# A transformer block on one core: weight splits ahead of the normalised input, the query's square ahead of the forget scan, and sums of squares two steps later

## The reference

```python
h = rms_norm(x, norm1_g)
z = h @ w_in                          # 512 pool, 512 q, 512 k, 512 v, 8 forget columns
log_f = log_sigmoid(z_f + b_forget)
q, k = rms_norm(q, q_norm_g), rms_norm(k, k_norm_g)       # per head, 8 heads of 64
y_pool = pool_mixer(z_pool, w_pool, pool_scale)           # trailing means over 2, 4, 8, 16 frames
F = cumsum(log_f, axis=1)
s = q @ k.T / sqrt(64) + F[t] - F[s]                      # causal, softmax, times v
x = x + concat([y_pool, y_attn]) @ w_out
x = x + peer_ffn(rms_norm(x, norm2_g), w_query, peer_sub_keys, expert_u, expert_v)
# peer_ffn: 8 retrieval heads, product keys, top 16 of 16384 experts per head,
# softmax gates, y = sum g_e * gelu(u_e . h) * v_e
```

## Time and profile before

| | |
|---|---|
| median of 3 runs | 1567.3 us (1561.99 to 1569.34) |
| span of the profiled execution | 1569.7 us; its time around the span is not listed apart |
| TensorE busy | 1513.6 us, 96% |
| DVE, ACT, POOL busy | 1156.7, 602.9, 973.6 us |
| mean granted clock of TensorE | 0.983 of full speed |
| chain that ended last | PE 79%, DVE 7%, ACT 5%, DMA 5%, issue 4%, POOL 1% |
| first 230 us | TensorE busy 200.1 us |

### The profile page before, as it was taken

How to read it: one execution, slowest core, us unless ns; L and a number is a source line. 1 busy time by engine, 2 the same in 40 slices (tenths; PEclk the granted TensorE clock), 3 DMA queues, 4 the chain that set the end, 5 groups by cost and what they waited for, 6 DMA issues and landing times.

```text
span 1569.7 us, 20625 instructions
## 1 busy us (share of the span) xinstructions
PE 1513.6 (96%) x7613; PEld 1323.5 (84%) x7613; DVE 1156.7 (74%) x1938; ACT 602.9 (38%) x808; POOL 973.6 (62%) x525
## 2 busy tenths in 40 slices
PE   6899999899999999999999999999999999999999
PEld 4655567688999999999899999998888888888887
DVE  5467754317899999819899889848777777777774
ACT  5557533433333333344343344433333333333332
POOL 2321133433578878666576667658878878888784
PEclk9899999999999999999999999999999999999999
DMA  4311111322467777568999998699888988888883
GB/s 154 108 67 47 49 54 68 118 77 81 144 214 251 271 262 258 197 223 276 352 334 334 357 361 300 236 355 396 325 348 318 348 348 316 350 322 343 348 296 121
DMA packets 117974, 381.53 MB, mean 243 GB/s; under 512 B 11416, under 2 KB 27928, under 8 KB 117408
## 3 DMA queue, kind: packets, MB, share of 16 engines
q1 hardware_dynamic: 70096, 202.64, 35.7%
q0 software_dynamic: 36864, 134.23, 23.3%
q10 hardware_dynamic: 10960, 44.06, 7.1%
HBM read 336.84 MB, written 44.06 MB: 243 GB/s over the span
## 4 chain that ended last, share of the span: by engine, by line
PE 79%; DVE 7%; ACT 5%; DMA 5%; issue 4%; POOL 1%; ACTq 0%; SPq 0%; DVEq 0%
PE bank L623 24%; PE bank L624 24%; PE bank L625 24%; DMA picked<-u_dram,picks 4%; PE bank L824 4%; ACT wh L428 1%; PE bank L768 1%; POOL wl L401 1%; DVE rinv L931 1%; DVE hl L884 1%; PE bank L639 1%; ACT L512 1%; DVE pr L1034 1%; DVE pad L1004 1%; PE bank L720 1%
## 5 line engine op out<-in xcount | busy, mean ns | idle before, releaser
L401 POOL TENSOR_TENSOR wl<-raw,wh 128x1024 fp32r<-128x1024 f32 x211 | 522.1, 2475 | 470.6 <-ACT wh L428 469.1
L623 PE MATMUL bank<-hh,wh 128*128 128x384 f32 (+1 forms) x1184 | 428.2, 362 | 7.1 <-DVE hl L884 7.1
L624 PE MATMUL bank<-hl,wh 128*128 128x384 f32 (+1 forms) x1184 | 415.4, 351 | 0.0
L625 PE MATMUL bank<-hh,wl 128*128 128x384 f32 (+1 forms) x1184 | 414.5, 350 | 0.0
L624 PE MATMUL bank<-wl,Wh 128*128 128x512 f32 x768 | 300.7, 392 | 0.0
L623 PE MATMUL bank<-wh,Wh 128*128 128x512 f32 x768 | 300.0, 391 | 0.0
L625 PE MATMUL bank<-wh,Wl 128*128 128x512 f32 x768 | 298.4, 389 | 0.0
L428 ACT ACTIVATE wh<-raw 128x1024 fp32r<-128x1024 f32 x225 | 236.7, 1053 | 151.7 <-PE bank L625 138.7
L623 PEld LDWEIGHTS bank<-hh,wh 128*128 128x128 f32 x1184 | 225.3, 190 | 17.1 <-DVE hl L884 7.4
L624 PEld LDWEIGHTS bank<-hl,wh 128*128 128x128 f32 x1184 | 225.4, 190 | 9.6 <-issue 1.7
L625 PEld LDWEIGHTS bank<-hh,wl 128*128 128x128 f32 x1184 | 224.8, 190 | 9.0
(11 more groups left out here) (164 smaller groups left out, 1759.7 us busy)
## 6 DMA issues: line engine op xcount, KB each, us to landing
raw<-uT_dram SPq DMA_DIRECT2D x128, 512.0 KB
xraw<-v_dram SPq DMA_DIRECT2D x72, 512.0 KB
raw<-v_dram SPq DMA_DIRECT2D x56, 512.0 KB
a_dram<-act_a ACTq DMA_DIRECT2D x64, 384.0 KB
wf<-a_dram SPq DMA_DIRECT2D x32, 768.0 KB, 6.9
raw<-wst_dram SPq DMA_DIRECT2D x41, 512.0 KB
gates_dram<-gbuf ACTq DMA_DIRECT2D x4, 4096.0 KB, 16.6
gt<-gates_dram SPq DMA_DIRECT2D x32, 512.0 KB
```

Source lines behind the costliest of these rows:

```text
L401: pool.tensor_tensor(wl[:, n % SPLIT, :], raw_of(n), wh[:, n % SPLIT, :].bitcast(F32), ALU.subtract).then_inc(w_lo, 1)
L623: pe.matmul(dst, ah, bh, start=start, stop=False)
L624: pe.matmul(dst, ah, bl, start=False, stop=False)
L625: return pe.matmul(dst, al, bh, start=False, stop=stop)
```

## The change

Three edits, in the list of steps and in ACT's program:

1. In `norm1`, ACT splits weight chunks up to 4 ahead of the first copy into `mh`, chunk 5 ahead of the fourth and chunk 6 ahead of the seventh; before, it had chunk 3 ahead of the fifth and chunks 4 to 6 behind the last. The numbers in `hi_to` are the last chunk to be split by then.
2. In a query or key chunk, ACT's square comes directly behind the copy, and only then the wait for the forget scan with its DMA (first chunk), or the wait for the stored rows with the loads of `nf` (second).
3. `ss` and `norm` of a chunk lie at pieces 2 and 3 of the next projection instead of 0 and 1.

```diff
         def sums(i):
 
-            return [(0, "ss", i), (1, "norm", i)]
+            return [(2, "ss", i), (3, "norm", i)]
...
                         act.activation(zc[:, z % 2, :], bank[bank_of(n)][:, :], ACT.Copy).then_inc(zc_ready, 1)
+                        if kind(n) == "qk":
+                            act.wait_ge(zc_ready, z + 1)
+                            square(SQ_QK + z, zc[:, z % 2, :])
                         if n == QK_W[0]:
                             act.wait_ge(f_done, 1)
                             act.dma_start(f_dram, fg[:, 2, :]).then_inc(f_stored, 16)
...
                             for h in range(2):
                                 forget(h)
-                        if kind(n) == "qk":
-                            act.wait_ge(zc_ready, z + 1)
-                            square(SQ_QK + z, zc[:, z % 2, :])
...
                     for k in range(KD):
-                        if what == "norm1" and k in (0, 4):
-                            hi_to(2 + k // 4)
+                        if what == "norm1" and k in (0, 3, 6):
+                            hi_to(4 + k // 3)
                         act.wait_ge(h_ready, base + k + 1)
```

## The result

The changed kernel takes 1580.4 us (median of 4 runs, 1579.3 to 1582.3), against 1568.3 for the kernel before: ratio 1.0078, interval 1.006 to 1.0097. It is slower by more than the 0.5% that can be told from no change, by some 12 us. The span of the profiled execution went from 1569.7 to 1580.5, +10.8, the mean granted clock from 0.983 to 0.978.

The account below looks back on a forecast made before the run. It took three chains, none TensorE's own, to decide; the heads' cycle closes on ACT and DVE. 0 - 4.9 + 2.0 + 1.1 + 7.8 + 0.8 = +6.8 on a 1569.7 span, 1576.5; as median 1574, range 1561 to 1583.

Parts of the forecast that it names:

- rival A: Heads: clock drops at the transposes make TensorE the bound; +12.3 us, about 1580, chance 0.24.
- Edit 1 brings nothing: First normalisation: four POOL meetings delay ml to 49.8, the forget scan ends as before, 0 us.
- The square ahead of the scan, the key 4.9 us sooner: Query and key chain: var starts right behind the scan, -3.5 us; -4.9 in all, key ready at 78.1.
- helps once more: Query and key chain: edit 3 lets the second var follow the first norm, key gain from 3.5 to 4.9 us.
- Half clock behind the first key, +2.0: First scores of head 0: a 3.8 us wait for the key brings half clock, costing 2.0 us.
- Head 0, +1.1: Head 0: the second mask is ready 0.6 us behind pT instead of 1.45, costing 1.1 us.
- Heads 1 to 4, +1.95 each: Heads 1 to 4: two Exps ahead of the table load delay root and norm 1.95 us each, +7.8.
- with a late sum behind a half clock: Upper end for the cost in heads 1 to 4: +3.0 us a head.
- 0.8 for all clock effects: Heads: clock drops from TensorE idling 2.3 us a head taken as +0.8 us in all, ends 0 and +7.
- waits for `pr` of about 2 us a head: Sign that the forecast is right: TensorE waits about 2 us a head for pr in heads 1 to 4.
- more than two half-clock stretches between 100 and 190 us: Sign in the trace that would make the outcome rival A.
- Behind the heads, no change: From head 5 on: order and lengths unchanged, so the shift goes through to the end.

Follow-up runs that it names:

- Experiment 4: Only the earlier weight splits in norm1, on the kernel before: 1569.6 us, ratio 1.0003.
- experiment 1: The changed kernel with sums and norms back at pieces 0 and 1, so edits 1 and 2 without edit 3: 1561.5 us, ratio 0.9969.
- experiment 5: The changed kernel with TensorE's sums back at piece 0, ACT and DVE keeping the late order: 1573.0 us, ratio 1.0033; a mirror kernel was run too.
- experiment 8: Two kernels with edits 1 and 2, late sums only for chunks 0, 1 and 3, or only in heads 0 to 4: 1564.1 and 1574.3 us.
- experiment 2: Only the sums and norms moved to pieces 2 and 3, on the kernel before: 1583.5 us, ratio 1.0098.
- the mirror of experiment 5: The changed kernel with TensorE's sums late at piece 2, but ACT and DVE in the order of before: 1574.4 us, ratio 1.005.
- the first of experiment 8: Edits 1 and 2, with late sums only for chunks 0, 1 and 3, outside and ahead of the heads: 1564.1 us, ratio 0.9985.
- experiment 7: Edits 1 and 2 with early sums, and the scaling of the values moved behind the forget projection: 1566.5 us, ratio 0.999.
- experiment 3: Only ACT's square moved directly behind the copy, on the kernel before: 1562.7 us, ratio 0.997.
- the second of 8: Edits 1 and 2, with late sums only in heads 0 to 4, those of chunks 0, 1 and 3 early: 1574.3 us, ratio 1.0067.

## Why the prediction was right and wrong

The time was in the range (1561 to 1583) and the direction was said, but the forecast, 1574 and "no change", was not what happened: rival A, slower by the clock, was, at the 1580 that it named, though mostly in other places than it said. That its number came out is in part luck: at head 5's Exp the kernel was 14.1 us late, where A had 12.3, and 3.4 came back behind it.

- *Edit 1 brings nothing.* Right. Four meetings with POOL, the last `ml` at 49.48 for 49.8, the scan at 60.84 for 61.4. Experiment 4 shows the zero by itself.
- *The square ahead of the scan, the key 4.9 us sooner.* Right, 5.6. But of this edit 3's share was taken as "helps once more", and beside edit 2 it doesn't: with early sums the key is ready at 77.27 to 77.73 (experiments 1, 5 and 8), with late ones at 77.24 to 77.38. Only without edit 2 does it bring 2.5 us (experiment 2). The copy right behind the split, which I counted for edit 3, comes of edit 2.
- *Half clock behind the first key, +2.0.* Place right, size wrong: +4.4. I put the stretch at 5 us of work at half clock, from the 6.8 us that stood in the trace of before; it was 20.5 us long. And it belongs to another edit than I thought, to TensorE's late sums. With early sums TensorE stands still for 1.44 us ahead of the second sum and 1.11 ahead of the key (the kernel with only ACT and DVE late); with late ones for 0.8 and 3.2, and the drop comes.
- *Head 0, +1.1.* The order alone costs 1.3 (experiment 5), the clock 3.1 more, which I had put at 0: under half clock the late sum keeps Ln waiting for `var` for 2.3 us.
- *Heads 1 to 4, +1.95 each.* Right in mechanism and size: 2.07 by the order alone, 8.3 in all for 7.8. The measured +11.0 from head 1's Exp to head 5's holds 2.7 more. For one of these cycles I can name it: 17.44 instead of 15.84, since the late sum has no slack left under half clock. The other 1.0 lies in the cycle to head 2's Exp, where half clock follows the wait for the second key; what it held there was not followed up. I had put "with a late sum behind a half clock" at +3.0 a head as an upper end, where that cycle measured +3.7, and then took 0.8 for all clock effects. The sign "waits for `pr` of about 2 us a head" did not come: they are 5.5 us in all (3.2 before), though TensorE idled 2.2 us of the cycle of 16.1, as forecast.
- *Rival A* had the drops come in the heads' idle at the transposes, and TensorE become the bound. Its sign, more than two half-clock stretches between 100 and 190 us, did come: they begin at 117.3, 151.5 and 185.6, where the kernel before has one. The wait for the second key was the 5.0 us that A gave it, and the first of the three follows it. But only one of heads 2 to 4 had a drop (151.5), and TensorE was not the bound there; the sum was late. Most of the clock's price was paid at the first scores and in head 0.
- *Behind the heads, no change.* 4.7 us came back in the output and expert parts and 1.3 were lost in heads 6 and 7, whose work is the same. For the heads the traces show the clock as the cause: the cycle to head 6's Exp takes 13.96 us with a 6.8 us stretch (before) and 12.20 where it is short or absent, the one to head 7's 16.65 next to without and 19.74 with one (changed). For the 4.7 us the clock is likely, but not shown. In the medians of the runs the difference is 12.1.

What failed is one term of the sum, the clock: 2.0 + 0 + 0.8 in the forecast for 4.4 + 3.1 + some 2.7 measured.

What stays open is why the clock stayed low for 17 to 20 us in a stretch in which TensorE was busy nearly throughout, where other stretches ended after 3.4 or 6.8 us of the same. The length of the wait alone does not set it: the waits for the second key, of 4.4 to 5.1 us in five kernels, were followed by 6.8 us each. The long stretch came in the three kernels with edit 2, TensorE's sums late ahead of head 0, and no filler (the changed one, the mirror of experiment 5, and the first of experiment 8), and in none of the others.

## What to carry to other kernels

- A wait of the busiest engine is worth nothing until one has followed what the engines behind it then do: here two chains on DVE, not TensorE's 4.8 us, set when the next thing could start. Look for the cycle that closes (from Exp to Exp without a gap on ACT and DVE), and put nothing into it, not even work that is done anyway beside it.
- Work moved later on one engine takes away slack that covered another's slow phases. Here the early sum is free cover against half clock, and its loss cost as much again as the order did.
- Test the edits of a bundle one at a time. Edit 2 alone, and edits 1 and 2 together, both at 0.997, beat both the kernel before and the changed one; edit 3 turned that into 1.008.

## What the runs showed of the hardware

- POOL's subtraction with two SBUF inputs and a DVE instruction with two SBUF inputs run one after the other. Where two subtractions were queued back to back, DVE's waiting instruction went in between them. POOL in the changed kernel:

```profile
28.89 5.51 POOL L401 TENSOR_TENSOR wl<-raw,wh 128x1024 fp32r<-128x1024 f32 x2 [2.43 <-ACT wh L428]
```

  `rinv` ended at 32.13, in the midst of this pair; the pair took 5.51 us, and four subtractions with no such DVE instruction beside them took 9.48 in the kernel before (from 43.67), 2.37 each.
- Half clock is not always short: 20.5 us at 0.50 with TensorE busy for 19.1 of them, against 3.4 to 6.8 us in all stretches of the kernel before and of eight of the ten experiments. A wait of 3.2 us for the key had it behind it in all three kernels (20.5, 20.5 and 17.1 us); one of 1.85 (experiment 7) had 6.8 us; those of 0.6, 1.07, 1.11, 1.54 and 1.76 us (experiments 1, 3, 5, the second of 8, and 2) had none. At the second key waits of 2.7 us and more were all followed by half clock (3.4 or 6.8 us, eight kernels), and those up to 1.3 us by none (four, one of them the kernel with spare matmuls).
